# 64 more prompt tokens moved from the dense expert phases to the gathered experts

## The chip, the cores and the metric

The kernel runs on one core of one Trainium2 chip. The metric is device time in microseconds (us) of one launch. Engines are named PE (TensorE), DVE (VectorE), ACT (ScalarE), POOL (GpSimd) and SP (SyncE, which only issues DMAs here). DMA queue q1 carries what SP issues, q10 what ACT issues, q0 the indirect gathers that POOL issues.

## The reference, cut to what matters

One decoder layer on 512 prompt tokens and 64 sample tokens: two parallel mixers (mLSTM and RWKV-7), an output projection, then a product-key expert layer ("peer") over 16384 experts, and a final norm. The mixers are untouched here. The expert layer is what the change works on:

```python
def block(xb):                                   # tokens after rmsnorm
    q = (xb @ w_q).reshape(PEER_BLOCK, PEER_HEADS, 2, PEER_QDIM // 2)
    s = jnp.einsum('bhpd,hpkd->bhpk', q, sub_keys)
    sv, si = lax.top_k(s, PEER_TOPK)             # 16 of 128 keys, 8 heads x 2 halves
    cand = sv[:, :, 0, :, None] + sv[:, :, 1, None, :]
    cv, ci = lax.top_k(cand.reshape(...), PEER_TOPK)
    idx = i1 * N_KEYS + i2                       # 8 heads x 16 picks = 128 experts of a token
    gate = jax.nn.softmax(cv, axis=-1)
    act = jax.nn.gelu(jnp.einsum('bhkd,bd->bhk', u_emb[idx], xb), approximate=False)
    return jnp.einsum('bhk,bhkd->bd', gate * act, v_emb[idx])
```

A token needs 128 rows of u and 128 rows of v, 1024 floats each. All is float32.

## The kernel before, in words

**Two ways to the same sum.** 448 of the prompt tokens (`DS`) go the dense way: every expert's dot product is computed for every one of them, and a gate that is zero for experts not picked weighs it. The last 64 prompt tokens and the 64 sample tokens, 128 together on the 128 partitions (tile 4 of `FTILES`), go the gathered way: for each of their 128 picks one indirect DMA fetches one row per partition (128 rows of 4 KB, 512 KB), and DVE multiplies and reduces it.

**Before the experts** (up to about 784 us) come the mixers, the output projection, the norm, the query projection and the key scores. Then two long phases follow.

**Dots phase.** 64 groups of 256 experts. A group's `u` (1 MB) is loaded by SP into one of two slots. ACT rounds it to `u_hi`, DVE forms the remainder `u_lo` (`split_u`), and PE does 2 x 24 matmuls with 448 columns (`dots`: hi*hi, hi*lo, lo*hi for eight depth slices, two tiles of 128 experts). ACT applies gelu and stores the result to a scratch in HBM. Beside it the gates of the dense tokens are made: DVE routes one tile of tokens at a time (`between` spreads the routing of the next tile over the groups of the present one), then builds one-hot rows for four tokens at a time, a quad (`one_hots`: per pair of quads one `hot_b`, one `hot_e`, two `hot_a`), PE turns a quad into 4 x 3 small matmuls (`gate_quad`), ACT copies it (`copy_quad`), and every eight quads 2 MB go to HBM. The order on every engine is written out by hand: 12 groups without gates (the head), then `GROUPS_OF` groups for tiles 0 to 3, then a tail of 3. `QUADS` says how many quads a group carries, `DOTS` how many gathered rows DVE works off at the end of a group (`sample_dot`, 128 in all). Matmuls with split operands need `u_lo`, so PE waits for DVE at each group and DVE for ACT's `u_hi`, which waits until PE has finished the group before the last.

**The gather ring.** POOL issues the gathers. They land in four buffers (`RING = 4`): gather number s waits until DVE has used row s - 4. So the fetch of a row can start only when the row four places ahead of it is done.

**Sum phase.** 32 groups of 512 experts. SP loads the stored activations, the gates (in pieces of 512 bytes) and `v` (2 MB) of a group into one of two slots, once DVE has split the group that had the slot. DVE multiplies activations and gates (`weights`), forms `v_lo` and `w_lo` (`split_v`, `split_weights`), ACT forms `v_hi` and `w_hi`, and PE adds 96 matmuls with 448 columns into eight banks (`sums`). `v_hi` of group g + 1 may be made only when `sums` of group g - 1 is done. Between these, DVE adds four gathered rows of `v` a group (`sample_add`), two before the splits and two after; this second row of gathers uses the same ring of four. After the last group the sums are turned back, added to the residual, normed and stored.

The lines that the steps touch are L2471 (`split_u`), L2477 (`sample_dot`), L2483 (`between`), L2502 (`one_hots`), L1825 (`dots`), L1912 (`sums`), L2684 to L2713 (the DVE helpers of the sum phase), L758 (`gather`).

Of the kernel before, what the change touches and what calls it, by code (L numbers as in the profile page):

```python
# [12 lines left out]
D = 1024  # L13
# [9 lines left out]
DS = SEQ - 64  # L23
FTILES = [(0, 128), (128, 128), (256, 128), (384, 64), (DS, 128)]
# [13 lines left out]
GROUPS_OF = [0, 16, 16, 13, 4]  # L38
# [10 lines left out]
assert DOT0[-1] + sum(TAIL_DOTS) == HEADS * TOPK  # L49
SLOTS = HEADS * TOPK  # L50
RING = 4
# [15 lines left out]
def hybrid_step(nc, xT_d, x_d, par_d, small_d, conv0_d, shift0_d, cn0_d, s0_d, w_in, w2_d, a2_d, g2_d,  # L67
# [11 lines left out]
    with ctx:  # L79
# [175 lines left out]
        sb("gap0", [128, KD * 64], scope=first)  # L255
# [4 lines left out]
        sb("gap1", [128, 2 * GU * 64], scope=first)  # L260
# [4 lines left out]
        xf = sb("xf", [128, 2, D], scope=norms)  # L265
# [3 lines left out]
        def xf_rows(t):  # L269

            return xf[:, t % 2, :] if t < 4 else xs[:, :]
# [26 lines left out]
        mx8 = sb("mx8", [128, 2, HEADS], scope=first)  # L298
        first.close()
# [5 lines left out]
        sb("gap2", [128, 256], scope=second)  # L305
# [3 lines left out]
        sb("gap3", [128, 512], scope=second)  # L309
# [3 lines left out]
        sb("gap4", [128, 448], scope=second)  # L313
        gring1 = sb("gring1", [128, NCH, GE, GC], scope=second)
        w_lo1 = sb("w_lo1", [128, GE, DS], f32r, scope=second)
        sb("gap5", [128, 512], scope=second)
# [15 lines left out]

        def pcol(name, t):
            return par[:, PCOL[name] + t:PCOL[name] + t + 1]
# [4 lines left out]
        s_out, s_tail = sem("stores_done"), sem("tails_stored")  # L339
# [95 lines left out]
        def _(sp):  # L435
# [32 lines left out]
            sp.dma_start(conv_o, conv_t[:, :, :, :]).then_inc(s_tail, 16)  # L468
# [17 lines left out]
            sp.dma_start(shift_o, shift_t[:, :, :]).then_inc(s_tail, 16)  # L486
            for p in range(4):
                if p == 2:
                    sp.wait_ge(S("chan_ready"), 4)
                    sp.wait_ge(s_tail, 32)  # L490
# [23 lines left out]
            sp.dma_start(subT[:, :, :], sub_d).then_inc(s_sub, 16)  # L514
            sp.wait_ge(S("x1_ready"), 10)
# [34 lines left out]
            for q in range(2):  # L550
                sp.wait_ge(s_gst[q], 16 * (NCH // 2 + 1))
# [5 lines left out]
            sp.wait_ge(S("row_used"), SLOTS)  # L557
# [16 lines left out]
            for t in ORDER:  # L574
                t0, n = FTILES[t]
                sp.dma_start(x1_late[t][0:n, :], x1_d[t0:t0 + n, :]).then_inc(s_x1, 16)
            for pos, t in enumerate(ORDER):
                t0, n = FTILES[t]
# [7 lines left out]
        def _(pool):  # L586
# [178 lines left out]
            for s in range(SLOTS):  # L765
                gather(s, rows_u[s % RING], pu_rows, "row_used")
# [2064 lines left out]
```

## Time and profile before

| | us |
|---|---|
| median of three timed runs | 2151.61 |
| the three runs | 2148.58, 2151.61, 2164.17 |
| span of the profiled execution, its own time from first to last instruction | 2149.9 |
| start of the dots phase on PE | about 784 |
| end of the head, first gates of tile 0 | about 912 |
| start of the sum phase on PE | 1511.4 |
| last sum on PE | 2137.0 |
| PE, DVE, ACT, POOL busy | 2046.7, 1532.6, 757.6, 609.0 |
| moved by DMA | 437.47 MB |

The phase marks are read from the trace in order of time. The page of the profile gives busy time by engine, the span in 40 slices, the DMA queues and the chain of work that ended last. The trace behind it can be asked for the instructions of one engine in order of time, for busy time in chosen stretches, and for the packets that each DMA queue moved in a stretch. A matmul's duration overlaps that of the next, so the pace of PE is read from a row that merges many of them, not from the mean of one. In the order of time, a row's bracket tells how long the engine stood idle before it and what it waited for.

### The profile page before, as it was taken

The page shows a single profiled execution, that of the slowest core. Times are in us where ns is not written, and L with a number is a line of the kernel's source. Part 1 is how long each engine was busy: PE and PEld are TensorE (multiplying, and loading weights), DVE is VectorE, ACT ScalarE, POOL GpSimd, SP SyncE. Part 2 cuts the span into 40 slices and gives each one's busy share as a digit, 9 for nine tenths or more (in the row PEclk, how much of TensorE's full clock was granted, in tenths as well). Part 3 has the DMA queues.
Part 4 walks back from the last instruction along what each step waited for, and adds up shares of the span by engine and source line. Part 5 has one row for each costly group of instructions (what it writes and reads, how often), then busy time and mean ns, then how long its engine had stood idle before and what let it go on. Part 6 is the DMA issues. An engine that isn't in the chain of part 4 may idle for free.

```text
span 2149.9 us, 35762 instructions
## 1 busy us (share of the span) xinstructions
PE 2046.7 (95%) x14513; PEld 1800.8 (84%) x14513; DVE 1532.6 (71%) x2662; ACT 757.6 (35%) x940; POOL 609.0 (28%) x515
## 2 busy tenths in 40 slices
PE   7999987788999998999999999999999999999997
PEld 7997866667447788998889889989999999999997
DVE  6526564776237899788898898897767666776676
ACT  5324443443021023345444544554322222222223
POOL 8144537450000000122332241212333233322330
PEclk9999988989999999999999999999999999999999
DMA  5112210011141214677887797779998888888873
GB/s 191 60 53 61 61 38 2 8 42 52 51 152 40 76 53 157 224 265 267 296 327 258 264 360 274 249 287 358 396 342 301 310 324 305 304 307 318 318 267 124
DMA packets 175772, 437.47 MB, mean 203 GB/s; under 512 B 12192, under 2 KB 92832, under 8 KB 165280
## 3 DMA queue, kind: packets, MB, share of 16 engines
q1 hardware_dynamic: 127552, 242.81, 32.5%
q0 software_dynamic: 36864, 134.23, 16.8%
q10 hardware_dynamic: 11232, 58.73, 6.7%
q8 instruction: 83, 1.36, 0.3%
q14 instruction: 41, 0.34, 0.0%
HBM read 368.57 MB, written 67.17 MB: 203 GB/s over the span
## 4 chain that ended last, share of the span: by engine, by line
PE 71%; DVE 10%; ACT 2%; issue 2%; POOL 2%; DMA 2%; ACTq 0%; DVEq 0%; POOLq 0%
PE bank L1923 29%; PE bank L1837 21%; PE bank L1742 3%; PE bank L1846 3%; PE bank L1820 3%; PE bank L1821 3%; DVE u_lo L2474 2%; DMA sca<-in_pu_rows,pick 2%; PE bank L1807 1%; DVE sca L2480 1%; PE bank L1787 1%; PE bank L1468 1%; PE bank L1379 1%; DVE isel L2609 1%; DVE hot_a L2532 1%
## 5 line engine op out<-in xcount | busy, mean ns | idle before, releaser
L1837 PE MATMUL bank<-xhi,u_hi 128*128 128x448 f32 x1008 | 379.6, 377 | 6.2 <-DVE u_lo L2474 6.2
L761 POOL DMA_INDIRECT sca<-in_pu_rows,pick x128 | 173.1, 1352 | 721.0 <-DVE sdot L2480 441.3
L1923 PE MATMUL bank<-w_hi,v_hi 128*128 128x448 f32 x1024 | 374.3, 365 | 0.6 <-ACT actb L1149 0.6
L1923 PE MATMUL bank<-w_lo,v_hi 128*128 128x448 f32 x1024 | 374.0, 365 | 0.0
L1923 PE MATMUL bank<-w_hi,v_lo 128*128 128x448 f32 x1024 | 374.0, 365 | 0.0
L1837 PE MATMUL bank<-xhi,u_lo 128*128 128x448 f32 x1008 | 369.4, 366 | 0.0
L1837 PE MATMUL bank<-xlo,u_hi 128*128 128x448 f32 x1008 | 368.6, 366 | 0.0
L761 POOL DMA_INDIRECT rows_v<-in_pv,pick x128 | 195.0, 1523 | 424.2 <-DVE xs L2689 373.5
L1202 ACT ACTIVATE v_hi<-v_raw 128x4096 fp32r<-128x4096 f32 x32 | 116.1, 3628 | 424.4 <-PE bank L1923 398.6
L2713 DVE TENSOR_TENSOR v_lo<-v_raw,v_hi 128x4096 fp32r<-128x4096 f32 x32 | 141.6, 4424 | 163.7 <-ACT v_hi L1202 163.7
L1837 PEld LDWEIGHTS bank<-xhi,u_hi 128*128 128x128 f32 x1008 | 189.6, 188 | 20.2 <-issue 6.5
L1923 PEld LDWEIGHTS bank<-w_hi,v_hi 128*128 128x128 f32 x1024 | 192.4, 188 | 16.2 <-ACT actb L1149 1.0
L1923 PEld LDWEIGHTS bank<-w_hi,v_lo 128*128 128x128 f32 x1024 | 192.4, 188 | 15.2
L1923 PEld LDWEIGHTS bank<-w_lo,v_hi 128*128 128x128 f32 x1024 | 192.4, 188 | 15.2
L1837 PEld LDWEIGHTS bank<-xhi,u_lo 128*128 128x128 f32 x1008 | 190.3, 189 | 17.4
L1837 PEld LDWEIGHTS bank<-xlo,u_hi 128*128 128x128 f32 x1008 | 190.2, 189 | 15.1
L1149 ACT ACTIVATE actb<-bank 128x448 f32<-128x448 f32 x128 | 69.7, 545 | 338.6 <-PE bank L1837 334.3
L2474 DVE TENSOR_TENSOR u_lo<-u_raw,u_hi 128x2048 fp32r<-128x2048 f32 x64 | 146.5, 2289 | 54.7 <-ACT u_hi L1124 54.2
L2689 DVE SCALAR_TENSOR_TENSOR xs<-rows_v,sdot,xs 128x1024 f32<-128x1024 f32 x127 | 162.7, 1281 | 14.5 <-DMA rows_v<-in_pv,pick 7.3
L2480 DVE CUSTOM_DVE_ANT_0 sca<-sca,xs 128x1024 f32<-128x1024 f32 x128 | 151.6, 1220 | 15.7 <-DMA sca<-in_pu_rows,pick 15.5
L1170 ACT ACTIVATE gst<-bank 128x512 f32<-128x512 f32 x112 | 125.3, 1147 | 17.6 <-PE bank L1846 14.3
L1124 ACT ACTIVATE u_hi<-u_raw 128x2048 fp32r<-128x2048 f32 x64 | 123.2, 1927 | 18.5 <-ACT gst L1170 8.6
(640 smaller groups left out, 3511.3 us busy)
## 6 DMA issues: line engine op xcount, KB each, us to landing
u_raw<-in_pu SPq DMA_DIRECT2D x64, 1024.0 KB
v_raw<-in_pv SPq DMA_DIRECT2D x32, 2048.0 KB, 16.9
act_scratch<-actb ACTq DMA_DIRECT2D x64, 448.0 KB
gate_scratch<-gst ACTq DMA_DIRECT2D x14, 2048.0 KB
wts<-act_scratch SPq DMA_DIRECT2D x32, 896.0 KB
gring<-gate_scratch SPq DMA_DIRECT2D x32, 896.0 KB
wring<-in_w_q SPq DMA_DIRECT2D x4, 2048.0 KB, 8.7
wp_raw<-in_w_in SPq DMA_DIRECT2D x7, 1024.0 KB, 6.6
```

The source lines that it names most:

```text
L761: pool.indirect_dma_start(dst, None, rows[:, :], bass.IndirectOffsetOnAxis(pick[:, s:s + 1], 0)).then_inc(s_row[s % RING], 16)
L1124: act.activation(u_hi[:, g % 2, :, :], u_raw[:, g % 2, :, :], ACT.Copy).then_inc(S("u_hi_ready"), 1)
L1149: act.activation(actb[:, q, e, :], bank[b][:, 0:DS], ACT.Gelu).then_inc(S("dot_banks_free"), 1)
L1170: act.activation(gst[:, c % 2, :, o:o + 4].rearrange("p a t -> p t a"), bank[5 + k % 2][:, :].rearrange("p (t a) -> p t a", t=4), ACT.Copy ...
L1202: act.activation(v_hi[g % 2][:, :], v_raw[g % 2][:, :], ACT.Copy).then_inc(S("v_hi_ready"), 1)
L1742: return mm(bank[jj % 6][0:n, :], mixT[:, kt, t0:t0 + n], w_o[:, half, kt, :], start=kt == 0, stop=kt == KD - 1)
L1837: ins = mm(bank[b][:, 0:DS], lhsT, rhs[:, 0:DS], **on)
L1923: ins = mm(bank[c][:, 0:DS], lhsT, rhs[q][:, e, :], **on)
L2474: TT(u_lo[:, g % 2, :, :], u_raw[:, g % 2, :, :], u_hi[:, g % 2, :, :].bitcast(f32), ALU.subtract).then_inc(S(f"u_lo_ready{g % 2}"), 1)
L2480: dve.tensor_tensor_reduce(rows_u[s % RING], rows_u[s % RING], xs[:, :], 1.0, 0.0, ALU.mult, ALU.add, sdot[:, s:s + 1]).then_inc(S("row_us ...
L2689: STT(out=accS[:, :], in0=rows_v[:, s % RING, :], scalar=sdot[:, s:s + 1], in1=accS[:, :], op0=ALU.mult, op1=ALU.add).then_inc(S("row_adde ...
L2713: TT(v_lo[q][:, :], v_raw[q][:, :], v_hi[q][:, :].bitcast(f32), ALU.subtract).then_inc(S("v_lo_ready"), 1)
```

## The change: what it does

The first 64 prompt tokens (`XT`) leave the dense way and go the gathered way too. Their 128 picks are spread over all 128 partitions: the 64 tokens lie there in two copies, one copy takes the first 64 picks of each token, the other the last 64. So they need 64 further gathers of 128 rows in each phase, 192 instead of 128 (`PAIRS`). The dense phases keep 384 tokens: three tiles of 128, 384 columns.

What it adds: SP copies the normed rows of these tokens twice (`few_x`); ACT issues four small copies of picks and gates (`few_pick`, `few_gate`) at the first group after the head; DVE computes the picks of the 64 tokens and a 128 x 64 selector (`few_sel`); DVE does 64 more dots (against `few_x`) and 64 more adds (into `few_sum`); PE adds the two copies up and into the banks by eight matmuls with that selector (`few_columns`) before the last two groups. What it removes: one of seven parts of the columns of each dense matmul, 16 of 112 quads with their gate copies, and a seventh of the bytes of activations and gates. What it moves: tile 0 is now the 64 gathered prompt tokens, routed first as before but with no quads; the 12 groups of that stage have dots only. `GROUPS_OF`, `QUADS` and `DOTS` are new. The loops of PE over the groups of two tiles are written out. The ring stays at four buffers.

```diff
-DS = SEQ - 64
-FTILES = [(0, 128), (128, 128), (256, 128), (384, 64), (DS, 128)]
+XT = 64
+XQ = 128 // XT
+DS = SEQ - 64 - XT
+FTILES = [(0, 64), (64, 128), (192, 128), (320, 128), (SEQ - 64, 128)]
...
-GROUPS_OF = [0, 16, 16, 13, 4]
+GROUPS_OF = [0, 12, 13, 13, 11]
...
-QUADS = [2] * 32 + [4 if j in (2, 6, 12) else 2 for j in range(13)] + [4] * 4
+QUADS = [0] * 12 + [4 if j in (2, 6, 10) else 2 for j in range(13)] * 2 + [2 + 2 * (j % 2) for j in range(11)]
...
-HEAD_DOTS, TAIL_DOTS = 6, [3, 2]
-DOTS = [5 if j in (13, 29) else 4 if j % 16 > 11 else 2 for j in range(32)] + [1 if q == 4 else 2 for q in QUADS[32:45]] + [3] * 4
+HEAD_DOTS, TAIL_DOTS = 8, [5, 4]
+DOTS = [5, 4] * 6 + [5 if j == 12 else 2 if QUADS[12 + j] == 4 else 3 for j in range(13)] * 2 + [5 if q == 2 else 3 for q in QUADS[38:49]]
...
+PAIRS = SLOTS + XT
+S_FIRST = 40
+DOT_ORDER = [("s", i) for i in range(S_FIRST)] + [("e", i) for i in range(XT)] + [("s", i) for i in range(S_FIRST, SLOTS)]
+ADD_ORDER = [("e", i) for i in range(XT)] + [("s", i) for i in range(SLOTS)]
 RING = 4
...
+            sp.wait_ge(S("xf_ready"), 1)
+            for c in range(XQ):
+                sp.dma_start(few_x[XT * c:XT * c + XT, :], xf_rows(0)[0:XT, :]).then_inc(s_copy, 16)
...
+            def few_columns():
+
+                pe.wait_ge(S("row_added"), XT)
+                for c in range(KD):
+                    mm(bank[c][:, DS:DX], few_sum[:, 128 * c:128 * c + 128], few_sel, start=False, stop=False,
+                       skip_group_check=True)
...
             def sample_dot(s):
 
+                kind, i = DOT_ORDER[s]
+                if s == S_FIRST:
+                    dve.wait_ge(s_copy, FEW_ROWS)
+                row, dot = (xs, sdot[:, i:i + 1]) if kind == "s" else (few_x, few_dot[:, i:i + 1])
...
+                for g in range(G0[pos], G0[pos] + GROUPS_OF[pos]):
+                    j = g - HEAD0
+                    quads = range(QUAD0[j], QUAD0[j + 1])
+                    for quad in quads[0:2]:
+                        quad_rows(quad)
+                    split_u(g + 1)
+                    for quad in quads[2:]:
+                        quad_rows(quad)
+                    for r in range(DOT0[j], DOT0[j + 1]):
+                        sample_dot(r)
+                    if pos < 4:
+                        between(pos, g - G0[pos])
...
-                for r in range(4):
-                    if r == (2 if g else 0) and g + 1 < EG:
+                adds = PAIRS // EG
+                for r in range(adds):
+                    if r == (adds // 2 if g else 0) and g + 1 < EG:
                         split_v(g + 1)
                         split_weights(g + 1)
-                    sample_add(4 * g + r)
+                    sample_add(adds * g + r)
```

**DVE, sum phase, one steady group.** An add of a gathered row is a SCALAR_TENSOR_TENSOR on `rows_v`; `wts`, `v_lo` and `w_lo` are the three preparing steps. Before:

```order
L2689 SCALAR_TENSOR_TENSOR xs<-rows_v,sdot,xs 128x1024 x2
L2700 TENSOR_TENSOR wts<-wts,gring 128x448 x4
L2689 SCALAR_TENSOR_TENSOR xs<-rows_v,sdot,xs 128x1024 x2
L2713 TENSOR_TENSOR v_lo<-v_raw,v_hi 128x4096
L2707 TENSOR_TENSOR w_lo<-wts,w_hi 128x1792
```

and now:

```order
L2747 SCALAR_TENSOR_TENSOR few_sum<-rows_v,few,few_sum 128x1024 x3
L2758 TENSOR_TENSOR wts<-wts,gring 128x384 x4
L2747 SCALAR_TENSOR_TENSOR few_sum<-rows_v,few,few_sum 128x1024 x3
L2771 TENSOR_TENSOR v_lo<-v_raw,v_hi 128x4096
L2765 TENSOR_TENSOR w_lo<-wts,w_hi 128x1536
```

Six adds stand in a group where four stood, three on each side of `wts`, and the three preparing steps keep their places.

**DVE, dots phase, the stage of tile 0.** An ISA row on `sca` is one dot with a gathered row, the ISA row behind it fetches its result; `hot` is a step of the routing of the next tile. Before, a group of this stage reads:

```order
L2525 TENSOR_TENSOR hot_b<-lanes,hk_ab 128x1024
L2528 TENSOR_TENSOR hot_e<-lanes,hk_ab 128x1024
L2532 TENSOR_TENSOR hot_a<-hot_e,hk_g 128x1536 x2
L2474 TENSOR_TENSOR u_lo<-u_raw,u_hi 128x2048
L2480 ISA sca,sdot<-sca,xs 128x1024
L2480 ISA sdot 128x1
L2480 ISA sca,sdot<-sca,xs 128x1024
L2480 ISA sdot 128x1
L2595 TENSOR_TENSOR hot<-cpos,lane 128x4096
L2603 TENSOR_TENSOR hot<-hot,sif 128x4096
```

and now, of a group with four dots:

```order
L2511 TENSOR_TENSOR u_lo<-u_raw,u_hi 128x2048
L2521 ISA sca,few<-sca,few_x 128x1024
L2521 ISA few 128x1
L2521 ISA sca,few<-sca,few_x 128x1024
L2521 ISA few 128x1
L2521 ISA sca,few<-sca,few_x 128x1024
L2521 ISA few 128x1
L2521 ISA sca,few<-sca,few_x 128x1024
L2521 ISA few 128x1
L2647 TENSOR_TENSOR hot<-cpos,lane 128x4096
L2655 TENSOR_TENSOR hot<-hot,sif 128x4096
```

The one-hot steps are gone from this stage, and four or five dots follow each other where there were two.

## Rows read from the trace of the kernel before

**Rows 1.** The page: span, and the chain that ended last.
```profile
span 2149.9 us, 35762 instructions
...
PE 71%; DVE 10%; ACT 2%; issue 2%; POOL 2%; DMA 2%; ACTq 0%; DVEq 0%; POOLq 0%
```

**Rows 2.** Windows: us; busy PE, PEld, DVE, ACT, POOL; granted clock, DMA share, GB/s.
```profile
787.00:912.40 125.40, 119.24 (x579) 109.02 (x579) 109.27 (x291) 40.67 (x42) 14.31 (x10) 0.97 0.53 180
912.40:1511.40 599.00, 594.77 (x3849) 535.24 (x3847) 520.18 (x795) 286.17 (x279) 158.81 (x118) 1.00 0.80 293
1530.00:1570.00 40.00, 40.00 (x199) 37.09 (x198) 31.71 (x27) 10.44 (x4) 20.13 (x12) 1.00 1.05 407
1600.00:2100.00 500.00, 500.00 (x2469) 463.45 (x2468) 344.15 (x259) 135.03 (x52) 158.36 (x104) 1.00 0.83 306
```

**Rows 3.** Chain in order of time: start us, us, what; 24 matmuls, 288 and 448 columns.
```profile
280.31 3.26 PE bank L1273 x24
...
912.34 4.91 PE bank L1837 x24
```

**Rows 4.** DVE in order of time, dots phase: a pair of quads, `split_u`, dots.
```profile
1084.60 0.69 DVE L2525 TENSOR_TENSOR hot_b<-lanes,hk_ab 128x1024 bf16<-128x1024 bf16 x1
...
1087.67 2.29 DVE L2474 TENSOR_TENSOR u_lo<-u_raw,u_hi 128x2048 fp32r<-128x2048 f32 x1
1089.88 1.22 DVE L2480 CUSTOM_DVE_ANT_0 sca<-sca,xs 128x1024 f32<-128x1024 f32 x1
...
1091.02 1.22 DVE L2480 CUSTOM_DVE_ANT_0 sca<-sca,xs 128x1024 f32<-128x1024 f32 x1
```

**Rows 5.** DVE: waits inside a group of five dots, and of the tail.
```profile
1067.40 1.23 DVE L2480 CUSTOM_DVE_ANT_0 sca<-sca,xs 128x1024 f32<-128x1024 f32 x1 [0.98 <-DMA sca<-in_pu_rows,pick]
...
1070.80 1.23 DVE L2480 CUSTOM_DVE_ANT_0 sca<-sca,xs 128x1024 f32<-128x1024 f32 x1 [0.93 <-DMA sca<-in_pu_rows,pick]
...
1073.60 1.23 DVE L2480 CUSTOM_DVE_ANT_0 sca<-sca,xs 128x1024 f32<-128x1024 f32 x1 [1.57 <-DMA sca<-in_pu_rows,pick]
...
1496.70 1.23 DVE L2480 CUSTOM_DVE_ANT_0 sca<-sca,xs 128x1024 f32<-128x1024 f32 x1 [6.46 <-DMA sca<-in_pu_rows,pick]
```

**Rows 6.** DVE in order of time, sum phase, one steady group.
```profile
1619.10 2.67 DVE L2689 SCALAR_TENSOR_TENSOR xs<-rows_v,sdot,xs 128x1024 f32<-128x1024 f32 x2
1621.68 2.22 DVE L2700 TENSOR_TENSOR wts<-wts,gring 128x448 f32<-128x448 f32 x4
1623.82 2.67 DVE L2689 SCALAR_TENSOR_TENSOR xs<-rows_v,sdot,xs 128x1024 f32<-128x1024 f32 x2
1632.12 4.42 DVE L2713 TENSOR_TENSOR v_lo<-v_raw,v_hi 128x4096 fp32r<-128x4096 f32 x1 [5.63 <-ACT v_hi L1202]
1636.46 2.02 DVE L2707 TENSOR_TENSOR w_lo<-wts,w_hi 128x1792 fp32r<-128x1792 f32 x1
```

**Rows 7.** POOL: the first gather issued in that group.
```profile
1620.64 1.93 POOL L761 DMA_INDIRECT rows_v<-in_pv,pick  x1 [11.72 <-DVE xs L2689]
```

**Rows 8.** DMA queues, 1618.9 to 1626 us: packets, MB, share of 16 engines.
```profile
q1 hardware_dynamic: 1688, 1.72, 77.8%
```

**Rows 9.** DMA queue of the gathers, 1620.6 to 1629.5 us, and the whole span.
```profile
q0 software_dynamic: 144, 0.55, 15.3%
...
q0 software_dynamic: 36864, 134.23, 16.8%
```

**Rows 10.** The same queue, 1620.6 to 1632.5 us.
```profile
q0 software_dynamic: 305, 1.13, 23.4%
```

**Rows 11.** DVE, sum phase: its first groups, then its last.
```profile
1535.35 1.28 DVE L2689 SCALAR_TENSOR_TENSOR xs<-rows_v,sdot,xs 128x1024 f32<-128x1024 f32 x1 [3.04 <-DMA rows_v<-in_pv,pick]
...
1545.21 1.28 DVE L2689 SCALAR_TENSOR_TENSOR xs<-rows_v,sdot,xs 128x1024 f32<-128x1024 f32 x1
...
2105.34 5.44 DVE L2689 SCALAR_TENSOR_TENSOR xs<-rows_v,sdot,xs 128x1024 f32<-128x1024 f32 x4
2113.95 2.68 DVE L2689 SCALAR_TENSOR_TENSOR xs<-rows_v,sdot,xs 128x1024 f32<-128x1024 f32 x2 [3.16 <-DMA rows_v<-in_pv,pick]
```

More of the change, by code:

```diff
@@ L22 @@
 TILES = [(t * 128, 128) for t in range(PT)] + [(SEQ, SAMP)]
-DS = SEQ - 64
-FTILES = [(0, 128), (128, 128), (256, 128), (384, 64), (DS, 128)]
+XT = 64
+XQ = 128 // XT
+DS = SEQ - 64 - XT
+FTILES = [(0, 64), (64, 128), (192, 128), (320, 128), (SEQ - 64, 128)]
+DENSE = slice(XT, XT + DS)
+DX = DS + XT
+LTILES = [(0, 128), (128, 128), (256, 128), (384, 64), (DX, 128)]
+PIECES = [[(0, XT + 128 * t, 128)] for t in range(3)] + [[(0, XT + 384, DS - 384)] * (DS > 384) + [(DS - 384, 0, XT)], [(0, DX, 128)]]
+NPIECES = sum(len(p) for p in PIECES)
 MCH = 128
@@ L298, in hybrid_step @@
         mx8 = sb("mx8", [128, 2, HEADS], scope=first)
+        few_x = sb("few_x", [128, D], scope=first)
+        pick0 = sb("pick0", [128, SLOTS], u32, scope=first)
         first.close()
@@ L1851, in _ @@
             pe.wait_ge(S("u_hi_ready"), 1)
-            for m, (u, x) in enumerate(((u_hi, xhi), (u_hi, xlo), (u_lo, xhi))):
+            x_low2 = xlo[:, :, DENSE]
+            for m, (u, x) in enumerate(((u_hi, xhi), (u_hi, x_low2), (u_lo, xhi))):
                 if m == 1:
@@ L1939, in _ @@
                     sums(i, 2 + q)
+            few_columns()
             sums(0, EG - 2)
@@ L2514, in one_hots, with quad_rows @@
                 link(TT(g2_, r, g1, ALU.subtract))
-                j = G0[pos] - HEAD0
-                for k in range(n // 4):
-                    quad = t0 // 4 + k
+                first_k, ahead = (XT // 4, 0) if t == 0 else (0, (t0 - XT) // 4)
+                if t == 0:
+                    link(dve.tensor_reduce(few_sel, ident[:, :].rearrange("p (c t) -> p t c", t=XT), AX.X, ALU.add))
+                def quad_rows(quad):
+                    k = quad - ahead + first_k
                     s = 2 * (quad % 4)
@@ L2674, in _ @@
             norm_gates(1, 0)
+            link(STT(out=cabf[0:XT, 0, :], in0=isel[0:XT, 0, :], scalar=128.0, in1=isel[0:XT, 1, :], op0=ALU.mult, op1=ALU.add))
+            dve.tensor_copy(pick0[0:XT, :], cabf[0:XT, 0, :]).then_inc(S("picked"), 1)
+            own(S("picked"))
             for s in range(4):
@@ L2684, in sample_add @@
             def sample_add(s):
[L2686 to L2687 removed]
+                kind, i = ADD_ORDER[s]
+                total, dot = (accS, sdot[:, i:i + 1]) if kind == "s" else (few_sum, few_dot[:, i:i + 1])
+                row = rows_v[:, s % RING, :]
+                dve.wait_ge(s_row[s % RING], 16 * ((PAIRS + s) // RING + 1))
+                if i:
                     dve.wait_ge(S("row_added"), s)
[L2689 to L2690 removed]
+                    STT(out=total[:, :], in0=row, scalar=dot, in1=total[:, :], op0=ALU.mult, op1=ALU.add
+                        ).then_inc(S("row_added"), 1)
                 else:
[L2692 removed]
+                    TS_(total[:, :], row, dot, None, ALU.mult).then_inc(S("row_added"), 1)
             def weights(g):
```

174 lines of the change are left out of this document (88 added, 86 removed).

## The prediction, made before the changed kernel ran

> **What bounds the kernel now.** I read the page first: PE holds 71% of the chain, DVE 10% [rows 1]. Then the stretches [rows 2]: from 912 us to the sum phase PE is busy 595 of 599 us and DVE 520; in the steady sum phase PE 500 of 500, DVE 344. So PE bounds both phases, but in the dots phase DVE has only 79 us to spare. The DMA engines are 0.80 and 0.83 busy, at 293 and 306 GB/s; where they are full they move 407 GB/s. The order in time shows where the slack lies: in a sum group DVE is idle once, 5.63 us, for `v_hi` [rows 6], which waits for PE. What the page doesn't show at all is the ring of four, since a gather is hardly ever waited for; I read it from POOL and the queues further down.
>
> **PE's gain.** 24 matmuls take 4.91 us at 448 columns and 3.26 us at 288 [rows 3], 205 and 136 ns each. On that line 384 columns cost 177 ns. A sum group takes 19.4 us now (32 groups in the 625.6 us from 1511.4 to 2137.0, some 4 us of it other work), 202 ns a matmul; at 384 columns 175 ns, 16.8 us. In the 599 us before it, 52 groups of 48 matmuls are 511 us and the 112 quads the other 88; now 442 us and 96 quads at 0.79 us, 76: 518 us. If PE stayed the bound, 81 us would go in the dots phase and 83 in the sum phase. All of it has to come through DVE and the ring.
>
> **DVE in the dots phase.** Dots follow each other at 1.14 us, a pair of quads takes 3.07 us [rows 4]. Of the 192 dots 8 lie in the head, so 184 follow where 122 did: 62 x 1.14 = +71 us. Sixteen quads less: 8 x 3.07 = -25 us. The shorter `wts` and `w_lo` of the first group and the selector cancel within 1 us. 520 + 71 - 25 = 566 us, against 518 on PE. DVE becomes the bound of this phase, in each stage and not only in the mean: with tile 0 (54 dots and no quads) as with the last (45 dots, 32 quads). The head gives nothing: DVE is busy in 109 of its 125 us and waits for two more rows there, while its xlo step shrinks by less than 1 us; so I leave its end at 912 us. At best the sum phase starts at 912 + 566 = 1478 us, 33 us earlier than now.
>
> **The ring in the dots phase.** The fetch for the fifth row of a burst starts when the first is done, three dots or 3.4 us before it is needed. The only rows where that is seen are the burst of five at 1065 us: waits of 0.98, 0.93 and 1.57 us, 3.5 in all [rows 5]. The bursts of four after it have none [rows 4]. The new table has fourteen bursts of five after the head (six with tile 0, one each with tiles 1 and 2, six with tile 3): 14 x 3.5 = 49 us. The bounds: nothing (a gather that lands within 3.4 us) and 6.5 us each (the wait in the tail, where activations, gates and `v` are loaded at once [rows 5]). I take 3.5, the same situation. In the tail nine dots stand where five did, beside those same loads; its one wait of 6.5 us comes again in part: 10 us, between 3 and 16. Since DVE is the bound, all of it counts. The sum phase starts at 1478 + 49 + 10 = 1537 us, 26 us later than now.
>
> **The sum phase, one steady group.** Count from the end of `w_lo`, when SP issues the next load. An add takes 1.29 us (two in 2.58 until `wts` starts, 1619.10 to 1621.68 [rows 6]). The first add ends at 1620.4, POOL issues at 1620.64 [rows 7]. But until 1626 only q1 moves anything: 1.72 MB, the activations and the gates in small pieces [rows 8]; of the gathers nothing. A gather is 144 packets (36864 for 256), and by 1629.5 the gather queue has moved 144 [rows 9]: landed 9.1 us after the add that freed its buffer. The next follows 2.6 us behind (305 packets by 1632.5, 288 are two [rows 10]). Today nobody needs that row for some 13 us: DVE has `wts`, two adds, its idle time and the splits before it, for the ring of four is exactly one group. With six adds a group it is two thirds of one. The row is needed after two more adds, `wts` and one add: 2.6 + 1.8 + 1.3 = 5.7 us. Activations and gates are a seventh shorter, which lets the gathers start 0.8 us sooner: 8.3 us. So the group reads:
> - first add ends 1.3, the fifth row lands at 9.6 (DVE ready at 7.0), added by 10.9;
> - the sixth row lands at 12.2, added by 13.5;
> - `v_lo` 4.34 and `w_lo` 1.66: 19.5 us.
>
> Without any wait it would be 15.6 us, and PE needs 16.8. The group takes 19.5 us, as long as today's 19.4, now paced by DVE and the ring. Bounds: 16.8 (PE) and 20.7 us (9.1 us to landing, 3.0 between landings). The bytes fit, but barely: 6 x 0.52 + 2.1 + 2 x 0.79 = 6.8 MB, 350 GB/s.
>
> [...]
>
> **Start and end of the sum phase.** The second group's end of `w_lo` lies 33.8 us after the start now (1545.2 [rows 11]); six adds instead of four before it and one more late row (3.0 + 1.1 us in [rows 11]) make it 40. Then 29 groups of 19.5, 566. After the last `w_lo`, at 2105.3, PE needed 31.7 us; now DVE has nine adds instead of six, and two rows late instead of one (3.16 [rows 11]), before it can empty the first banks, and PE waits for that: 36. The norm and the store stay at 13. `few_columns`, eight small matmuls, falls into PE's idle time; without that it would cost 2 us. The copies of `few_x`, picks and gates are six DMAs long before their use. POOL issues 64 more gathers a phase at 1.5 to 2.2 us, idle most of the time today. Together 40 + 566 + 36 + 13 = 655 us.
>
> **Sum.** 1537 + 655 = 2192 us on the profiled execution, whose span of 2149.9 lies 1.7 us under the median. So **2194 us**, 42 slower.
>
> **The rivals.**
> 1. As above, the ring runs dry at the fifth row in both phases: 2194, by itself 2165 to 2225. Chance 0.6.
> 2. [...] 0.08.
> 3. **Half of it**: in the quiet end the row freed at 2106.6 was waited for until 2113.95 [rows 11], 7.3 us. With that in every group 18.5 us, and 2 us a burst of five: start at 1478 + 28 + 5 = 1511, then 38 + 537 + 34 + 13: 2133, with the offset 2135. 0.2.
> 4. **The queues fill up** since more is asked of them: 20.7 us a group, 18 us more in the dots phase: 1555 + 42 + 600 + 38 + 13 = 2248, 2250. 0.12.
>
> That narrower matmuls don't run faster is no case of its own: at today's 19.4 us PE would still need no more than DVE.
>
> **The numbers.** The predicted time is that of the first case. 1% of 2152 us, 22 us, is what I count as telling a change from none: under 2130 faster, over 2173 slower. Faster: the second case, and of the third a third, 0.15. Within 1%: the rest of the third and 0.05 of the first, 0.18. Slower: 0.67. The range leaves out the second case and the outer parts of the third and fourth: 2120 to 2250.
>
> **What would show it.** In the changed profile: PE no longer at 500 of 500 us in the sum phase but near 430, with a gap each group before `sums` for `w_lo`; adds of DVE waiting for `rows_v` twice a group, at the fifth and sixth place after `w_lo`, some 2.5 and 1.3 us; a group of 19 to 20 us; in the dots phase PE waiting for `u_lo`, and waits for gathers at the fifth dot of a burst; the start of the sum phase between 1510 and 1560. It would be wrong if the sum group took under 18.5 us, that is, if the first gather after a load landed within 7 us, or if the bursts of five showed no waits.

## The result, and the profile after

Four runs of the changed kernel gave 2275.35, 2285.93, 2288.09 and 2288.43 us, median 2287.0; four of the kernel before, on the same chip, a median of 2152.9. The ratio is 1.061, 95% interval 1.057 to 1.065: 134 us slower, where 42 were predicted. The profiled execution has a span of 2286.2 us, so 94 us above the 2192 of the sum.

The page: the chain of work that ended last, 71% PE before [rows 1], is now mostly DVE and transfers.

```profile
span 2286.2 us, 35606 instructions
...
DVE 32%; DMA 21%; PE 19%; issue 11%; POOL 5%; ACT 2%; ACTq 0%; DVEq 0%; POOLq 0%
```

The windows (columns as in [rows 2]): the head, the rest of the dots phase up to the first sum, and the same 500 us of the sum phase.

```profile
787.00:920.00 133.00, 114.26 (x622) 111.03 (x622) 118.66 (x305) 41.88 (x45) 16.09 (x12) 0.94 0.51 179
920.00:1572.80 652.80, 546.27 (x3635) 525.64 (x3633) 562.22 (x881) 260.75 (x262) 241.76 (x181) 0.92 0.83 305
1600.00:2100.00 500.00, 423.76 (x2206) 416.40 (x2205) 356.22 (x280) 118.98 (x47) 251.12 (x140) 0.91 0.87 317
```

No engine is full anywhere: PE 424 of 500, DVE 356, and the DMA engines move 317 GB/s, where full they moved 407 [rows 2]. That is the picture of a wait that goes round in a circle: DVE waits for a row, PE waits for DVE, and the next fetch waits for the buffer that DVE still holds. The waits name it, DVE's and then PE's (us in total, times, longest):

```profile
DVE xs L2747 <- DMA rows_v<-in_pv,pick: 123.0, 42, 5.7
...
DVE few_sum L2747 <- DMA rows_v<-in_pv,few: 62.3, 20, 5.6
...
DVE sca L2521 <- DMA sca<-in_pu_rows,few: 13.9, 7, 6.0
```
```profile
PE bank L1959 <- DVE w_lo L2765: 93.8, 30, 5.4
PE bank L1873 <- DVE u_lo L2511: 56.7, 16, 10.3
```

One steady sum group of DVE in order of time, which answers to [rows 6]:

```profile
1719.74 4.06 DVE L2747 SCALAR_TENSOR_TENSOR few_sum<-rows_v,few,few_sum 128x1024 f32<-128x1024 f32 x3
1723.72 1.96 DVE L2758 TENSOR_TENSOR wts<-wts,gring 128x384 f32<-128x384 f32 x4
1725.60 1.27 DVE L2747 SCALAR_TENSOR_TENSOR few_sum<-rows_v,few,few_sum 128x1024 f32<-128x1024 f32 x1
1732.50 1.28 DVE L2747 SCALAR_TENSOR_TENSOR few_sum<-rows_v,few,few_sum 128x1024 f32<-128x1024 f32 x1 [5.63 <-DMA rows_v<-in_pv,few]
1735.14 1.28 DVE L2747 SCALAR_TENSOR_TENSOR few_sum<-rows_v,few,few_sum 128x1024 f32<-128x1024 f32 x1 [1.36 <-DMA rows_v<-in_pv,few]
1736.35 4.42 DVE L2771 TENSOR_TENSOR v_lo<-v_raw,v_hi 128x4096 fp32r<-128x4096 f32 x1
1740.68 1.75 DVE L2765 TENSOR_TENSOR w_lo<-wts,w_hi 128x1536 fp32r<-128x1536 f32 x1
```

The two waits are where the prediction put them, at the fifth and the sixth row; the sixth has its predicted size. The fifth is 5.6 us here and 4.8 in the mean of 28 groups, not 2.6, and the group 21.8 us, not 19.5. The dots phase shows the same kind of wait at the fifth dots of two bursts, one in the stage with tile 0 and the last before the tail, to hold against [rows 5]:

```profile
955.04 1.23 DVE L2521 CUSTOM_DVE_ANT_0 sca<-sca,xs 128x1024 f32<-128x1024 f32 x1 [5.97 <-DMA sca<-in_pu_rows,pick]
...
1542.34 1.23 DVE L2521 CUSTOM_DVE_ANT_0 sca<-sca,xs 128x1024 f32<-128x1024 f32 x1 [9.50 <-DMA sca<-in_pu_rows,pick]
```

### The profile page after: what moved, and what is told of

Its sections match the earlier page's. It is cut to its first block, busy times and chain, and to the rows that moved or that the text cites. A ratio compares the mean times of both kernels' runs of the same rounds, so it can differ in the third digit from the quotient of the medians.

```text
span 2286.2 us, 35606 instructions
## 1 busy us (share of the span) xinstructions
PE 1960.9 (86%) x14337; PEld 1792.4 (78%) x14337; DVE 1642.1 (72%) x2826; ACT 729.3 (32%) x925; POOL 838.8 (37%) x643
## 3 DMA queue, kind: packets, MB, share of 16 engines
q0 software_dynamic: 55296, 201.35, 23.7%
## 4 chain that ended last, share of the span: by engine, by line
DVE 32%; DMA 21%; PE 19%; issue 11%; POOL 5%; ACT 2%; ACTq 0%; DVEq 0%; POOLq 0%
DMA rows_v<-in_pv,pick 9%; DVE sca L2521 6%; DMA sca<-in_pu_rows,pick 5%; DMA rows_v<-in_pv,few 5%; DVE u_lo L2511 5%; DVE hot_a L2577 3%; PE bank L1778 3%; POOL rows_v L786 3%; DVE w_lo L2765 2%; PE bank L1856 2%; PE bank L1857 2%; DVE xs L2747 2%; PE bank L1873 1%; DVE few_sum L2747 1%; DMA sca<-in_pu_rows,few 1%
## 5 line engine op out<-in xcount | busy, mean ns | idle before, releaser
L1959 PE MATMUL bank<-w_hi,v_hi 128*128 128x384 f32 x1024 | 366.9, 358 | 93.8 <-DVE w_lo L2765 93.8
L1873 PE MATMUL bank<-xhi,u_hi 128*128 128x384 f32 x1008 | 361.3, 358 | 56.8 <-DVE u_lo L2511 56.7
L1959 PE MATMUL bank<-w_lo,v_hi 128*128 128x384 f32 x1024 | 361.5, 353 | 0.0
L1959 PE MATMUL bank<-w_hi,v_lo 128*128 128x384 f32 x1024 | 360.6, 352 | 0.0
L1873 PE MATMUL bank<-xlo,u_hi 128*128 128x384 f32 x1008 | 352.9, 350 | 0.0
L1873 PE MATMUL bank<-xhi,u_lo 128*128 128x384 f32 x1008 | 350.7, 348 | 0.0
L786 POOL DMA_INDIRECT rows_v<-in_pv,pick x128 | 231.3, 1807 | 226.6 <-DVE xs L2747 202.0
L1176 ACT ACTIVATE actb<-bank 128x384 f32<-128x384 f32 x128 | 62.7, 491 | 352.3 <-PE bank L1873 335.0
L786 POOL DMA_INDIRECT rows_v<-in_pv,few x64 | 109.2, 1707 | 122.3 <-DVE few_sum L2747 94.0
L786 POOL DMA_INDIRECT sca<-in_pu_rows,few x64 | 86.2, 1347 | 143.5 <-DVE few L2521 124.8
## 6 DMA issues: line engine op xcount, KB each, us to landing
v_raw<-in_pv SPq DMA_DIRECT2D x32, 2048.0 KB, 19.2
```

The costliest lines, as they stand in the source:

```text
L786: pool.indirect_dma_start(dst, None, rows[:, :], bass.IndirectOffsetOnAxis(at, 0)).then_inc(s_row[s % RING], 16)
L1176: act.activation(actb[:, q, e, :], bank[b][:, 0:DS], ACT.Gelu).then_inc(S("dot_banks_free"), 1)
L1873: ins = mm(bank[b][:, 0:DS], lhsT, rhs, **on)
L1959: ins = mm(bank[c][:, 0:DS], lhsT, rhs[q][:, e, :], **on)
```

## The experiments

The table is read from DVE's order of time in each trace: end of the first `w_lo` (PE starts the sums there), waits for rows from the head's end to that point, the mean of 28 steady sum groups, and the waits for rows in one of them, all in us. Names that begin with s change the sum phase, those with d the dots phase, those with c both. Every kernel was run four or five times beside 4 to 9 runs of the kernel before, whose medians were 2151.6 to 2152.9 us.

| kernel | median us | ratio to before, 95% | sums start | row waits, dots phase | sum group | row waits in it |
|---|---|---|---|---|---|---|
| before | 2152.9 | | 1510.8 | 14 | 19.3 | 0 |
| changed | 2287.0 | 1.057 to 1.065 | 1572.8 | 79 | 21.8 | 6.2 |
| s_no_fetch | 2121.2 | 0.981 to 0.989 | 1563.7 | 75 | 16.5 | 0 |
| d_no_fetch | 2202.3 | 1.019 to 1.025 | 1488.4 | 0 | 22.0 | 6.3 |
| s_ring6 | 2133.4 | 0.986 to 0.994 | 1569.5 | 78 | 16.7 | 0 |
| s_ring5 | 2137.2 | 0.992 to 0.997 | 1569.2 | 79 | 16.6 | 0.9 |
| s_spread | 2234.3 | 1.034 to 1.045 | 1561.2 | 73 | 19.8 | 4.2 |
| s_values_first | 2273.0 | 1.050 to 1.058 | 1573.9 | 82 | 21.2 | 5.5 |
| s_small_loads | 2134.7 | 0.992 to 0.996 | 1564.1 | 75 | 16.5 | 0.7 |
| s_big_pieces | 2263.1 | 1.047 to 1.054 | 1569.3 | 81 | 21.0 | 5.4 |
| d_ring5 | 2259.1 | 1.042 to 1.051 | 1548.4 | 56 | 21.8 | 6.2 |
| d_even | 2267.8 | 1.047 to 1.058 | 1544.1 | 58 | 22.0 | 6.4 |
| d_small_u | 2265.3 | 1.046 to 1.056 | 1544.6 | 55 | 21.9 | 6.3 |
| c_rings_even | 2092.0 | 0.969 to 0.974 | 1524.1 | 36 | 16.7 | 0 |
| c_balanced | 2070.6 | 0.962 to 0.967 | 1500.0 | 7 | 16.6 | 0 |

The kernels whose dots phase is that of the changed one start the sums between 1561 and 1574 us, with waits of 73 to 82 us: so far apart can single traces of one and the same phase lie.

**What the rows cost: s_no_fetch and d_no_fetch.** All dots and adds stay, 188 of 192 gathers of one phase go. Here the sum phase; DVE's wait for a row is relaxed to match.

```diff
-            for s, which in enumerate(ADD_ORDER):
+            for s, which in enumerate(ADD_ORDER[0:RING]):
                 gather(s, which, rows_v[:, s % RING, :], pv, "row_added")
```

> The changed kernel without 188 of the 192 gathers of the sum phase: DVE does all 192 adds, on the four rows that the first four gathers brought (the sums of the gathered tokens are left out in this way). Theory A (rows are the only thing waited for): PE sets the pace at 16.8 us a group at a granted clock of 1.0; 29 x 5.0 = 145 us less and some 8 us at start and end: about 2135 us (2125 to 2150). Theory C (narrower matmuls or the lower clock bound the phase beside the rows): PE stays at a clock near 0.9, 18.7 us a group, 2190 or more.

> The changed kernel without 188 of the 192 gathers of the dots phase: DVE does all 192 dots on four rows (the activations of the gathered tokens are left out in this way; the sum phase is unchanged). In the changed kernel DVE waits 79 us for rows between the end of the head and the sum phase, and 5.6 us in the head. Theory A (DVE bounds the phase, so every such wait counts): the sum phase starts at 1573 - 85 = 1488 us, the time is about 2202 us (2190 to 2215). Rival (PE or the loads of u take the waits' place): DVE waits for u_hi instead, less than 50 us gained, 2237 or more.

Measured 2121 and 2202 us: 166 us less in the sum phase, 4 us under the expected range, since a group takes 16.5 us and not 16.8 and the sums start 9 us earlier in the trace, and 85 less in the dots phase, as expected to the microsecond. PE at 384 columns runs at a granted clock of 1.00 and is busy all the time (499.3 us of the 500 from 1600 to 2100 in s_no_fetch). The narrower matmuls do give what they promised; the fetching of rows takes it back. The two savings together, 251 us, would leave 2036 us (an estimate, the two were not run as one), beside 2037, which the prediction's numbers give if no row is ever late: 1478 at the start of the sum phase, 2 that I put for the hand-over to PE, 32 x 16.8 + 4, 13 at the end and 2 of offset.

**The ring: s_ring6 and s_ring5.** The tiles of the sum phase have become narrower, so the gaps between them now hold whole rows of 4 KB per partition.

```diff
-        sb("gap3", [128, 4096 - 2 * GE * DS], scope=second)
+        row_v4 = sb("row_v4", [128, D], scope=second)
...
-        sb("gap5", [128, 9920 - 5 * GE * DS - D], scope=second)
+        row_v5 = sb("row_v5", [128, D], scope=second)
+        sb("gap5", [128, 9920 - 5 * GE * DS - 2 * D], scope=second)
```

> The changed kernel with six buffers instead of four for the rows of the sum phase (one whole group of rows), nothing else. In the changed kernel a steady sum group takes 21.8 us: 15.6 us of DVE work, 4.8 us of waiting for the fifth row after w_lo and 1.4 us for the sixth. Theory A (the ring of four is too short for six rows a group): both waits go, PE is the bound at 16.8 us a group; the same 6.8 MB a group then need 405 GB/s, as much as the fullest stretch moved, so 17 to 18 us a group, 29 x 4.2 = 120 us less than the changed kernel's 2287: 2150 to 2180 us, and PE's granted clock back at 1.0 in the sum phase. Theory B (the DMA engines are the bound: they are 0.86 busy at 313 GB/s in the sum phase, more buffers ask for nothing else): the group stays above 20.5 us and the time above 2250.

> The changed kernel with five buffers for the rows of the sum phase alone (four gave 21.8 us a group with 6.2 us of waits, six gave 16.7 and none). Theory A: the row whose fetch starts with the first add after w_lo is then the sixth, needed 8.4 us after w_lo and landing 12.0 us after it: one wait of 3.6 us, 19.2 us a group, 29 x 2.6 = 75 us less: about 2212 us (2195 to 2225). Rival (the fetches share the DMA engines, so with five outstanding each takes longer): 20.5 us a group or more, 2250 or more.

Six buffers: 2133 us, 154 less than four, below the 2150 to 2180 expected of theory A, since a group takes 16.7 us and not 17 to 18, and 1% under the kernel before. A steady 100 us of it, columns as in [rows 2]:

```profile
1700.00:1800.00 100.00, 100.00 (x579) 100.00 (x578) 92.38 (x72) 30.54 (x14) 67.05 (x37) 1.00 1.04 411
```

PE is full again, at full clock, and the DMA engines move 411 GB/s instead of 317: theory B, that they were the bound at 0.87, has fallen. For five buffers both theories had the group too slow: it took 16.6 us, not 19.2, and has one wait of 0.9 us where 3.6 us were expected. The row fetched first after the load landed 12.7 us after `w_lo` in the group of the changed kernel above; with five buffers it lands 9.3 us after it, though more goes beside it. SP's issues and DVE's wait in a group of s_ring5, whose `w_lo` ends at 1888.6:

```profile
1888.84 0.34 SPq L564 DMA_DIRECT2D wts<-act_scratch  x1
...
1889.92 7.26 SPq L561 DMA_DIRECT2D v_raw<-in_pv  x1
```
```profile
1897.90 1.28 DVE L2750 SCALAR_TENSOR_TENSOR xs<-rows_v,sdot,xs 128x1024 f32<-128x1024 f32 x1 [0.88 <-DMA rows_v<-in_pv,pick]
```

Why it lands sooner stays open. SP takes 7.3 us to issue the values here, 0.8 to 1.6 in the changed kernel, so one could think that the values enter the engines later and the rows meet less beside them. Two figures speak against that: in the first 9.3 us after `w_lo` SP's queue moves 2.2 MB here and 1.8 in the changed kernel, and s_spread below has such long issues too (7.9 us in the median) while its row lands only after 11.3 us. A fifth buffer did buy more than one row's time.

**Order against depth: s_spread, d_even, d_ring5.** s_spread and d_even keep the ring of four and spread the need for rows, d_ring5 adds a fifth buffer in the dots phase. The edits of s_spread and of d_even:

```diff
s_spread
-                    weights(g + 1)
-                adds = PAIRS // EG
-                for r in range(adds):
-                    if r == (adds // 2 if g else 0) and g + 1 < EG:
+                    if g:
+                        weights(g + 1)
                         split_v(g + 1)
+                        sample_add(adds * g)
+                        sample_add(adds * g + 1)
                         split_weights(g + 1)
...
+                for r in range(2 if g + 1 < EG else 0, adds):
                     sample_add(adds * g + r)
d_even
+                    early = DOT0[j] + (DOT0[j + 1] - DOT0[j]) // 2
...
-                    for r in range(DOT0[j], DOT0[j + 1]):
+                    if pos < 4:
+                        for r in range(DOT0[j], early):
+                            sample_dot(r)
+                        between(pos, g - G0[pos])
+                    for r in range(early, DOT0[j + 1]):
                         sample_dot(r)
-                    if pos < 4:
-                        between(pos, g - G0[pos])
```

> The changed kernel with the same ring of four and the same fetches, but DVE works in another order in the sum phase: after w_lo four adds, wts, v_lo, two adds, w_lo (now three adds, wts, three adds, v_lo, w_lo). The fifth row is then needed 11.5 us after the end of w_lo instead of 7.1; it lands about 12.0 us after it. Theory A (latency of the ring): the wait shrinks to about 0.5 and 1.4 us, 17.5 us a group, 29 x 4.3 = 125 us less: about 2165 us (2150 to 2190). Theory B (bytes or queue): what is asked for sooner lands later by as much, the group stays above 20.5 us, 2250 or more.

> The changed kernel with the ring of four, but each group's dots stand in two parts of at most three, with the routing of the next tile between them (in the last stage u_lo and quads), instead of in one burst of up to five. The prediction's picture (only the fifth row of a burst is late, since its fetch starts with the burst): nearly all waits go, 60 us or more gained, about 2222 us. Theory A (ring of four gives four rows in 11.2 us however they are spread): nothing to be had with tile 0, where rows are wanted all the time, some 20 us in the last stage, where five and three dots alternate: about 2265 us (2255 to 2280).

> The changed kernel with five buffers instead of four for the rows of the dots phase alone. Theory A (a ring of n gives n rows in the time from a row's release to its successor's landing): in the stage with tile 0 nine dots come in 18.2 us of DVE's work and now take 25.1 us, four rows in 11.2 us; five rows in 11.2 us make 20.2 us, so 5 us less for each of six pairs of groups, and most of the waits of the last stage and the tail go: 40 to 55 us less than 2287, about 2240 us (2230 to 2250). Rival (the fetches share the DMA engines, so with five outstanding each takes longer): less than 20 us gained, 2267 or more.

s_spread missed: 19.8 us a group, not 17.5. I had looked only at the row that was late. With four adds after `w_lo`, the fourth needs the row whose buffer came free 1.7 us before `w_lo` ended. POOL, busy with the gather before it, issued that fetch 0.5 us before the end (1933.75), 0.8 us ahead of the load, and still the row was late:

```profile
1942.22 1.29 DVE L2747 SCALAR_TENSOR_TENSOR xs<-rows_v,sdot,xs 128x1024 f32<-128x1024 f32 x1 [3.94 <-DMA rows_v<-in_pv,pick]
```

d_even came out at the expected time for the wrong reason. With tile 0, where theory A saw nothing to gain, the waits fell from 34.9 to 24.5 us; in the last stage and the tail from 38.8 to 29.4. d_ring5 did less than expected: 28 us, its waits with tile 0 fell to 23.7 and not to some 12. So neither picture alone holds in the dots phase: not the burst's (spreading would have removed nearly all) nor that of a fixed time per fetch (five buffers would have gained twice as much). The traces tell what became of the rest, for they keep the time at which each row landed (how, is told below): with tile 0 a row landed 8.1 us after its buffer came free with four buffers, and 9.5 us after it with five. That is what the rival of d_ring5 said, that each fetch takes longer with five out, and it goes with a gain about half of what was expected.

**What a late row is made of.** Four kernels with other loads. Of s_small_loads the values are shown; its activations and gates are made as small in the same way.

```diff
s_values_first
+                    load_values(q, pv_g[g].squeeze(0))
                     load_acts(q, act_d[g].squeeze(0))
                     load_gates(q, gate_v[g].squeeze(0))
-                    load_values(q, pv_g[g].squeeze(0))
s_small_loads
-                    load_values(q, pv_g[g].squeeze(0))
+                    sp.dma_start(v_raw[q][:, 0:256], pv_g[g].squeeze(0)[:, 0, 0:256]).then_inc(s_v[q], 16)
s_big_pieces
-                    load_gates(q, gate_v[g].squeeze(0))
+                    sp.dma_start(gring[q][:, :, :, :].rearrange("p c e t -> p (c e t)"), act_d[g].squeeze(0)).then_inc(s_grp[q], 16)
d_small_u
-                    sp.dma_start(u_raw[:, q, :, :], pu[bass.ds(i * 2 + (2 + q), 1)].squeeze(0)).then_inc(s_u[q], 16)
+                    sp.dma_start(u_raw[:, q, 0:1, :], pu[bass.ds(i * 2 + (2 + q), 1)].squeeze(0)[:, 0:1, :]).then_inc(s_u[q], 16)
```

> The changed kernel, but SP issues the values (2 MB in pieces of 4 KB) of a group before its activations and gates; the gates come in pieces of 512 bytes. In the trace nothing moves on the gather queue for some 6 us after the load is issued, while activations and gates go. Theory A1 (the many small pieces ahead are what keeps the gathers back): gathers now go beside the values at once, the fifth row lands 3 us sooner or more, 18.5 us a group, about 2195 us. Theory A2 (the gathers wait for what was issued ahead of them, whatever its pieces): no gain, within 15 us of 2287, or slower as the gates come last and wts waits for them.

> The changed kernel with the ring of four, but from the third sum group on each load brings little: 48 KB of activations, 16 KB of gates and 128 KB of values in place of 0.77, 0.77 and 2 MB (the rest of the sums is left out in this way); all six gathers a group stay. In the changed kernel the fifth row lands 12.0 us after w_lo, 10.7 us after the add that freed its buffer. Theory Q (most of these 10.7 us are the load that stands ahead): rows land some 4 us after their buffer is free, DVE waits for none, PE sets the pace at 16.5 us a group, about 2140 us (2125 to 2155). Theory L (a gather takes about 10 us whatever goes beside it): the waits stay, the group stays above 20 us, 2240 or more.

> The changed kernel, but in the steady sum groups the 0.77 MB of gates, read in pieces of 512 bytes, are replaced by 0.77 MB read in pieces of 6 KB (the wrong bytes, so the gates are left out in this way); queue, order and bytes are the same. In the changed kernel the gather queue moves nothing from 1.5 to 7.8 us after w_lo, and from 4 us on q1 goes through these small pieces. Theory P (the small pieces keep the gathers back): the fifth row lands 2.5 us sooner or more, the group takes 19.3 us or less, 2215 us or less. Theory S (the gathers are that late by their own start after POOL's issue, and then share the engines with the values): less than 1 us a group, 2260 or more.

> The changed kernel with 128 KB instead of 1 MB in each of SP's loads of u from the third group on (the rest of the dot products is left out in this way); all gathers stay. DVE waits 85 us for rows in the head and the dots phase. Theory Q (the rows are late because the loads of u, 1 MB a group, share the engines): most of the waits go, 60 us less or more, 2227 us or less. Theory L (a gather's own time from release to landing fills the ring of four where 9 rows are wanted in 18 us): less than 30 us less, 2257 or more. Between these both count.

The gather queue in the changed kernel, counted from 1719.8 us, the end of `w_lo`: up to 1726.7, 1727.3, 1729.4 and 1732.4 us (packets, MB, share of 16 engines). This answers to [rows 8 to 10].

```profile
q0 software_dynamic: 137, 0.50, 21.4%
...
q1 hardware_dynamic: 1339, 1.50, 69.8%
q0 software_dynamic: 152, 0.56, 21.7%
...
q0 software_dynamic: 279, 1.05, 29.4%
...
q0 software_dynamic: 485, 1.79, 36.7%
```

The first 137 packets are the rest of the gathers of the group before; the last of them moves at 1721.8. Then the queue stands still until 1726.8, 5.5 us after POOL's issue at 1721.3. At 1729.4 the next 144 packets are all but through, a gather's worth, 9.6 us after `w_lo`, as predicted; and the prediction called that the landing. But DVE goes on only at 1732.50, and by then 348 packets have moved, 2.4 gathers' worth. The count of packets does not say whose they are.

For the late row they run from 1728.8 to 1732.48, and DVE goes on at 1732.50. The second row's first step comes at 1730.2, long before the first row's last: several gathers are in the engines at once, and a row is there only with its sixteenth step.

In s_small_loads POOL issues the same gather at 1699.83 us; counted from 1698.4, the end of `w_lo`, the queue stands at 152 by 1702.7 and at 311 by 1705.4. The last step that the trace keeps of that row comes at 1705.0, and it is no longer waited for; the next one is, for 0.55 us.

```profile
q0 software_dynamic: 152, 0.56, 46.7%
...
q0 software_dynamic: 311, 1.14, 58.2%
```
```profile
1707.35 1.28 DVE L2747 SCALAR_TENSOR_TENSOR few_sum<-rows_v,few,few_sum 128x1024 f32<-128x1024 f32 x1 [0.55 <-DMA rows_v<-in_pv,few]
```

The means over the same 28 groups, for the row fetched first after `w_lo`: without a load beside it the first packet moves 2.6 us after POOL's issue and the row lands 2.7 us later, 6.7 us after `w_lo`. In the changed kernel the first packet moves 5.5 us after the issue and the row lands 4.8 us after that, 11.8 us after `w_lo`. So the load costs some 3 us before the first packet and 2 behind it. In s_big_pieces, without the small pieces, the first packet still moves 5.4 us after the issue, and the row lands at 11.0: the small pieces are not what holds the start back. The group gains 0.8 us and the time is 2263 us, which is theory S, close to its edge. Issuing the values first was worth 0.6 us a group and 14 us in all, theory A2. s_small_loads came out as theory Q had it (2135 us): most of the lateness is the load. What keeps the queue still for 5.5 us is open: it goes with a full load beside it, but neither the small pieces nor the order of the load explain it.

d_small_u gained 22 us, theory L: with tile 0 the waits fell from 34.9 to 19.2, in the last burst and the tail they stayed (16.6 after 15.5). So two thirds of the waits of the dots phase (55 of 79 us) are there without the loads of `u`.

The quickest of the 256 gathers of the kernel before took 4.1 us, counted from the start of POOL's issue to the last step, and those of s_small_loads that follow `w_lo` take 5.2 us in the mean, with next to nothing on the other queues (0.20 MB on SP's from 1698.4 to 1707.3 us). Of the 6.4 us from the release of the next row's buffer (1700.9) to its landing (1707.3), 1.1 us are POOL still issuing the gather before it.

**Both rings and the dots: c_rings_even and c_balanced.** The first joins s_ring6, d_ring5 and d_even. The second has a sixth buffer in the dots phase too and moves dots to the stages that wait for nothing:

```diff
-HEAD_DOTS, TAIL_DOTS = 8, [5, 4]
-DOTS = [5, 4] * 6 + [5 if j == 12 else 2 if QUADS[12 + j] == 4 else 3 for j in range(13)] * 2 + [5 if q == 2 else 3 for q in QUADS[38:49]]
+HEAD_DOTS, TAIL_DOTS = 8, [4, 0]
+DOTS = [4] * 12 + [3 + (j in (3, 6, 9, 12)) for j in range(13)] + [3 + (j in (2, 4, 7, 9, 12)) for j in range(13)] + [5 if q == 2 else 3 for q in QUADS[38:49]]
```

> Both in one: six buffers in the sum phase, five in the dots phase, and the dots in two parts. With six buffers in the sum phase alone the time was 2133 us. Theory A: 79 us of waits for rows in the dots phase shrink to 15 to 30, so 2133 - 55 = 2078 us (2065 to 2095), and the DMA engines stay at 410 GB/s in the sum phase. Rival (DVE's work or PE takes the place of the waits): above 2105.

> Six buffers in both phases, the dots in two parts, and the dots moved from the stage with tile 0 (54 to 48) and from the tail (9 to 4) to the stages of tiles 1 and 2, where no row is waited for. With six, five and the old table the time was 2092 us, of which 15.5 us were waits for rows with tile 0, 9.8 in the last stage and 10.9 in the tail. Theory A: these 36 us shrink to 10, about 2066 us (2055 to 2078). Rival (PE or the first loads of the sum phase take the waits' place): above 2082.

c_rings_even: 2092 us, 14 above the middle of what was expected and within its range, with 36 us of waits left. c_balanced: 2070.6 us, in its range too, 82 under the kernel before and 216 under the changed one. Its dots phase and 400 us of its sum phase:

```profile
908.50:1500.00 591.50, 535.05 (x3666) 513.90 (x3665) 563.60 (x889) 262.41 (x262) 256.16 (x179) 0.97 0.92 341
1600.00:2000.00 400.00, 400.00 (x2310) 400.00 (x2309) 372.88 (x291) 122.30 (x50) 282.61 (x146) 1.00 1.04 411
```

DVE is busy 564 of 592 us in the one, PE always in the other. These are the bounds that the 2037 us above are added up from, DVE in the dots phase and PE in the sum phase; the time came to 2070.6.

## Why the prediction was wrong, step by step

**The mechanism held.** The ring runs dry at the fifth and sixth row, DVE paces both phases, PE idles: 424 of 500 us, where "near 430" was named. The likeliest case was the one that came, on the predicted side, but the time lies 37 us above the top of the range.

**PE's gain** was right: 16.5 to 16.7 us a group once rows are there, 172 to 174 ns a matmul.

**DVE in the dots phase** was right: 562 us busy against 566.

**The end of the head** was put at 912 and came at 920. The two dots that waited there cost 5.6 us; the prediction named their wait and still left the end where it was.

**The ring in the dots phase** was too small: the fourteen bursts of five waited 71 us, 5.1 each and not 3.5. The burst of [rows 5] stood among groups with two and four dots. (It was not the only one, as the prediction says: a second burst of five at 1248.6 us waited 3.5 us too, among the same neighbours.) With tile 0 fives and fours follow each other, and the ring starts each burst without its lead; there it was 5.8 each, and 1.9 in the two bursts among threes. In the last stage 5.5, with the 9.5 us shown above beside the first load of the values. The tail had 6 us instead of 10. With the rest (u_hi 2.5, PE 1.1, and gaps too short to be named) the sum phase began at 1573 us, not at 1537: 36 of the 94 us.

**The steady sum group** is the step that failed: "by 1629.5 the gather queue has moved 144 [rows 9]: landed 9.1 us after the add that freed its buffer". The 144 packets came when predicted; they were no landing. In the kernel before no one waited for that row, so no wait showed its landing, and I took the count for it; even the upper bound (9.1 us, 3.0 between) was built on the count. The landing was in the trace all the same. The semaphore steps of the very row of [rows 9] run from 1628.2 to 1631.1 us: it landed 10.7 us after the add that freed its buffer, not 9.1, and the next one 2.6 us behind, as predicted. In the mean of 28 groups that row landed 12.0 us after `w_lo` in the kernel before and 11.8 in the changed one. So the change did not make it later, it only made it wanted; and the 0.8 us that the prediction took off for the shorter loads were 0.2. In the prediction's own sum, 12.0 us in place of 9.6 give a group of 21.9 us; measured were 21.8.

The wait for the fifth row became 4.8 us instead of 2.6, that for the sixth 1.36 as predicted (1.3), the rest 15.6 as predicted. 28 groups of 21.8 instead of 19.5 are 64 us; the last of the 29 groups (16.5) and the start (38.4, not 40) were 5 us shorter than their terms. The norm (13) and the 36 us after the last `w_lo` were right. That leaves the other 58 us of the 94.

**The rivals.** No late row (the second case, 2037 us): s_ring6 shows that the 16.8 us a group of this case were right; the ring of four came near it only with the loads taken away (s_small_loads). The half (7.3 us to landing): it was read from an end that was not quiet. SP issues loads of the residual there at 2103.5 us, and its queue moves 2.0 MB from 2106 to 2114; so the 7.3 us are neither the time beside a group's load (10.7) nor the time without one (5.4 in s_small_loads, from the release of the first row's buffer to its landing). Full queues, 20.7 us: nearest in size, but not the mechanism, for the row landed no later than in the kernel before, and the same engines moved 411 GB/s with six buffers.

**The gap on the gather queue.** The 5.4 us from POOL's issue at 1620.64 [rows 7] to 1626, without a packet of the gathers [rows 8], were read as the load shutting them out. The runs soften that: 2.6 us of such a gap are there without a load. The rest is not cleared up; once the gathers have begun, both queues move side by side (in the changed kernel q0 1.23 MB and q1 0.87 MB from 1727.3 to 1732.4 us).

## What to carry to other kernels

A ring of n buffers is a number of rows in flight, not a number of rows at hand: before more rows are put into a period, count how many are freed and wanted between one load and the next, and price each by the time from the buffer's release to the landing that someone waited for. Packets that have moved on a queue are no landing when several transfers are out on it (here a gather's worth by 1729.4 us, the landing at 1732.48). Where no wait shows a landing, look for the steps of the semaphore that the transfer raises, which the trace of the kernel before already held; without them the packet count is only a lower bound. And when no engine is full and DMA is at 0.87, look for a circle of waits before calling it bandwidth: here one more buffer, in room that the change itself had freed, turned 6% slower into 0.6% faster (2137 us, interval 0.992 to 0.997).

## What the runs showed of the hardware

The clock: PE pauses in each steady sum group, between 1.2 and 5.4 us, 3.1 us in the one shown (1716.8 to 1719.9), and in 25 of the 28 groups the granted clock is at 0.50, the lower of the two levels in this trace, for a stretch at or near the restart. Here it is 0.50 from 1721 to 1722, the window from 1720 has 0.57, a mix of both levels, and the next one is back at 1.00. Windows of the changed kernel, last columns as in [rows 2]:

```profile
1716.00:1720.00 4.00, 0.93 (x6) 0.61 (x5) 4.00 (x3) 1.38 (x1) 2.97 (x1) 1.00 0.37 129
1720.00:1724.00 4.00, 4.00 (x15) 4.00 (x16) 3.79 (x4) 2.24 (x1) 2.40 (x2) 0.57 0.84 235
1724.00:1728.00 4.00, 4.00 (x25) 4.00 (x25) 2.87 (x5) 1.49 (x1) 2.57 (x3) 1.00 1.01 339
```

PE is busy 18.6 us in a group (521.7 us in 28) instead of 16.6. It cost nothing here, since DVE and the rows set the 21.8 us.

POOL's issue of a gather in a sum group takes 0.9 to 1.9 us, but where it falls beside `v_lo`, 4.9 us. POOL, changed kernel:

```profile
1734.06 0.93 POOL L786 DMA_INDIRECT rows_v<-in_pv,few  x1 [5.98 <-DVE few_sum L2747]
1736.70 4.87 POOL L786 DMA_INDIRECT rows_v<-in_pv,few  x1 [1.71 <-DVE few_sum L2747]
```

It ends 0.8 us after `v_lo`, and the same stands in all 28 groups. Whether that delay matters was not tried, and what holds the issue up beside `v_lo` is not shown.

The DMA engines show 1.04 busy and 411 GB/s for 400 us on end in c_balanced, against 407 in [rows 2] for 40 us: at that rate PE was never kept waiting.
